# A hybrid decoder layer on one core: the per-layer-embedding product computed between the router's matmuls and kept in DRAM scratch, and the last expert pair scattered into four PSUM banks

## The reference, cut to what matters

```python
mix = jnp.concatenate([h_m, h_b], axis=-1) @ w_out[l]
x = x + mix
y = moe_ffn(rmsnorm(x, ffn_norm_g[l]), w_router[l], b_router[l], w_gate_up[l], b_gate_up[l], w_down[l], b_down[l])
x = x + y
g = jax.nn.sigmoid(rmsnorm(x, ple_norm_g[l]) @ w_ple_gate[l])
x = x + g * (p[l] @ w_ple_proj[l])

# in moe_ffn
logits = t @ w_router + b_router
top_vals, top_idx = lax.top_k(logits, 4)
gates = one_hot(top_idx) weighted by softmax(top_vals)
for e in range(32):
    hu = t @ w_gu[e] + b_gu[e]
    glu = min(hu[:, :1024], 7);  lin = clip(hu[:, 1024:], -7, 7)
    y = y + gates[:, e:e+1] * ((glu * sigmoid(1.702 * glu) * (lin + 1)) @ w_dn[e] + b_dn[e])
```

## Time and profile before

| | |
|---|---|
| three timed runs | 1172.05, 1172.11, 1172.97 us (median 1172.11) |
| profiled execution, span from first to last instruction | 1169.2 us (its own time outside the span is not recorded) |
| PE busy, share of the span | 1120.5 us, 96% |
| DVE, ACT, POOL busy | 235.3, 159.4, 20.1 us |
| bytes moved by DMA | 431.36 MB |
| chain that ended last, by engine | PE 70%, DMA 26%, DVE 1%, ACT 1%, POOL 1% |

### The profile page before, as it was taken

The page is one execution under the profiler, slowest core; times in us unless marked ns, Lnnn a source line. Parts: engine busy times, 40 slices in busy tenths (PEclk is TensorE's granted clock), DMA queues, the critical chain, the costliest instruction groups (busy, mean ns, idle before and its releaser), DMA issues.

```text
span 1169.2 us, 12153 instructions
## 1 busy us (share of the span) xinstructions
PE 1120.5 (96%) x5234; PEld 451.5 (39%) x5234; DVE 235.3 (20%) x478; ACT 159.4 (14%) x308; POOL 20.1 (2%) x44
## 2 busy tenths in 40 slices
PE   6999997999999999999999989999989899999898
PEld 3476554343434343434334333333333333333243
DVE  2364134111111111202111201111111111111021
ACT  3223313110100000001101010100000000000031
POOL 2000110000000000000000000000000000000000
PEclk9999988999999999999999999999999999999999
DMA  9932426899999999999999999999999999999940
GB/s 351 317 135 82 159 93 252 317 428 427 427 428 428 426 428 428 427 429 426 428 427 429 426 426 429 428 428 427 428 428 427 428 429 425 428 429 427 425 193 36
DMA packets 41214, 431.36 MB, mean 369 GB/s; under 512 B 5728, under 2 KB 5984, under 8 KB 16584
## 3 DMA queue, kind: packets, MB, share of 16 engines
q1 hardware_dynamic: 41104, 430.54, 88.0%
q10 hardware_dynamic: 56, 0.03, 0.0%
HBM read 429.51 MB, written 1.05 MB: 368 GB/s over the span
## 4 chain that ended last, share of the span: by engine, by line
PE 70%; DMA 26%; DVE 1%; ACT 1%; POOL 1%; issue 0%; POOLq 0%; DVEq 0%; ACTq 0%
DMA ring<-in_w_gate_up 26%; PE hu L837 24%; PE po L858 14%; PE aux L813 5%; PE hu L532 5%; PE aux L822 3%; PE hu L538 2%; PE hu L547 2%; PE hu L829 2%; PE po L850 2%; PE po L967 1%; PE hu L967 1%; PE po L844 1%; PE po L675 0%; PE aux L789 0%; PE po L894 0%
## 5 line engine op out<-in xcount | busy, mean ns | idle before, releaser
L837 PE MATMUL hu<-ring,xg_t 128*64 128x512 f32 x2048 | 466.5, 597 | 23.3 <-DMA ring<-in_w_gate_up 23.3
L837 PEld LDWEIGHTS hu<-ring,xg_t 128*64 128x64 f32 x2048 | 137.7, 136 | 329.8 <-issue 284.2
L858 PE MATMUL po<-ring,early 128*64 128x512 f32 x1024 | 226.8, 595 | 0.0
L858 PEld LDWEIGHTS po<-ring,early 128*64 128x64 f32 x1024 | 70.7, 137 | 153.9 <-issue 130.8
L1255 DVE TENSOR_SCALAR early<-hu 128x512 f32<-128x512 f32 x32 | 22.1, 692 | 463.6 <-PE hu L837 463.6
L1241 DVE TENSOR_TENSOR xt<-xt,aux 128x512 f32<-128x512 f32 x68 | 43.7, 684 | 164.5 <-PE aux L822 164.5
L822 PE MATMUL aux<-num_t,early 64*128 64x512 f32 x272 | 67.6, 615 | 0.3 <-ACT num_t L1502 0.3
L532 PE MATMUL hu<-ring 128*128 128x512 f32 x144 | 63.9, 596 | 0.0
L813 PEld LDWEIGHTS aux<-early,big 128*128 128x128 f32 x512 | 58.4, 192 | 13.0 <-issue 13.0
L813 PE MATMUL aux<-early,big 128*128 128x128 f32 x512 | 61.4, 278 | 0.0
L1494 ACT ACTIVATE early<-early 128x512 f32<-128x512 f32 x32 | 20.2, 630 | 254.0 <-DVE early L1255 254.0
(11 more groups left out here) (249 smaller groups left out, 553.9 us busy)
## 6 DMA issues: line engine op xcount, KB each, us to landing
ring<-in_w_gate_up SPq DMA_DIRECT2D x128, 2048.0 KB, 34.5
ring<-in_w_down SPq DMA_DIRECT2D x64, 2048.0 KB, 36.7
ring<-in_w_in SPq DMA_DIRECT2D x7, 2048.0 KB, 15.5
ring<-in_w_out SPq DMA_DIRECT2D x2, 2048.0 KB, 8.3
ring<-in_w_ple_gate SPq DMA_DIRECT2D x2, 2048.0 KB, 37.0
xt<-in_x SPq DMA_DIRECT2D x2, 512.0 KB, 4.1
ring<-in_w_ple_proj SPq DMA_DIRECT2D x1, 1024.0 KB, 34.0
out_x<-big SPq DMA_DIRECT2D x4, 256.0 KB, 2.0
```

Source lines behind the costliest of these rows:

```text
L837: last = mm(hu[n * SLOTS:(n + 1) * SLOTS, 2 * e + b, :], xg[:, k, e * SLOTS:(e + 1) * SLOTS], w[:, o:o + NB], start=(k == 0), stop=(k == K ...
L858: last = mm(po[n * SLOTS:(n + 1) * SLOTS, 0, :], actT[:, f, h * SLOTS:(h + 1) * SLOTS], w[:, o:o + NB], start=False, stop=(h == 1 and f == ...
```

## The change

1. `p` is transposed right after `output_transposes(1)`, into `aux`, and ScalarE copies it to SBUF (`pT`).
2. SP loads `w_ple_proj` right behind expert chunk 6 into the SBUF tile that had held the mLSTM numerators; to make it fit, `num_t` and `xg_t` become one tile `num_xg`, with the same contents at the same use.
3. `ple(0)` to `ple(3)` run between the router's matmuls, into the `hu` banks; ScalarE copies each to SBUF (`ple_s`), and SP stores the two tiles to a DRAM scratch of 1 MB behind expert chunk 8. The first up chunk waits for the four copies, the first activation for the stores.
4. At the end the order of the last loads is the two `w_ple_gate` chunks, then the scratch (1 MB) in the place of `w_ple_proj`; VectorE reads the product from there.
5. The first pair has no scatter, and GpSimd's two memsets are gone.
6. The last pair is scattered inside the loop, tile 0 into `aux` and tile 1 into `hu`, so that tile 1 no longer waits for VectorE. The gate product goes into `aux` and `hu` (`GATE_BANKS`), and its waits are split: the first four matmuls for ScalarE's columns, the next four for VectorE's.
7. ScalarE's squares and column copies at the end are interleaved.

```diff
@@ -171,8 +171,9 @@
         actT = early[:, 3072:3072 + NB].rearrange("p (f s) -> p f s", s=P)
-        out_s = num_t[:, 0:2 * NB].rearrange("p (e n) -> p e n", e=2)
-        pT = early[:, 1536:1536 + PLE // P * S].rearrange("p (k s) -> p k s", s=S)
+        out_s = num_xg[:, 0:2 * NB].rearrange("p (e n) -> p e n", e=2)
+        pT = early[:, 768:768 + PLE // P * S].rearrange("p (k s) -> p k s", s=S)
+        ple_s = [early[:, 2560:2560 + D], early[:, 1536:1536 + D]]
@@ -340,12 +343,16 @@
-        PLE_BANKS = [hu[:, 0, :], hu[:, 1, :], aux[:, 0, :], aux[:, 1, :]]
+        GATE_BANKS = [aux[:, 0, :], aux[:, 1, :], hu[:, 0, :], hu[:, 1, :]]
...
+
+        ple_d = nc.dram_tensor("ple_scratch", (S, D), F32).ap()
+        ple_dst = ple_d.rearrange("(t p) d -> t p d", p=P)
+        ple_src = ple_d.rearrange("(t p) d -> p t d", p=P)
@@ -398,6 +405,12 @@
                 load_expert(m)
+                if m == 6:
+                    sp.dma_start(w_pp, w_pp_k).then_inc(wpp_loaded, 16)
+                if m == RING - 1:
+                    for tt in range(TT):
+                        sp.wait_ge(ple_ready, HALVES * (tt + 1))
+                        sp.dma_start(ple_dst[tt, :, :], ple_s[tt]).then_inc(ple_stored, 16)
@@ -409,8 +422,10 @@
                         load_expert(m)
-            for c, (parts, src) in enumerate(((PLE // P, w_pp_k), (4, w_pg_k[:, 0:4, :]), (4, w_pg_k[:, 4:8, :]))):
+            for c, (parts, src) in enumerate(((4, w_pg_k[:, 0:4, :]), (4, w_pg_k[:, 4:8, :]), (TT, ple_src))):
                 sp.wait_ge(chunk_done, npass * PER_PASS + (MOE0 + c - RING + 1))
+                if c == 2:
+                    sp.wait_ge(ple_stored, 16 * TT)
@@ -494,10 +509,6 @@
-
-            pool.wait_ge(chunk_done, CHUNK_WO_A + 1)
-            g.memset(ghotT, 0.0).then_inc(ghotT_ready, 1)
-            g.memset(out_s, 0.0).then_inc(out_s_ready, 2)
@@ -736,6 +747,10 @@
             output_transposes(1)
+            for k in range(PLE // P):
+                for tt in range(TT):
+                    last = tr(aux[:, 1, k * S + tt * P:k * S + tt * P + P], pt_in[:, tt, k * P:(k + 1) * P], ident[:])
+            last.then_inc(pT_ps, 1)
@@ -757,6 +772,17 @@
+            def ple(q):
+
+                tt, n = divmod(q, HALVES)
+                if q == 0:
+                    pe.wait_ge(wpp_loaded, 16)
+                pe.wait_ge(xq_ready, q + 1)
+                for k in range(PLE // P):
+                    last = mm(hu[:, q, :], pT[:, k, tt * P:(tt + 1) * P], w_pp[:, k, n * NB:(n + 1) * NB],
+                              start=(k == 0), stop=(k == PLE // P - 1))
+                last.then_inc(ple_ps, 1)
@@ -764,17 +790,20 @@
             for q in range(2):
-                pe.wait_ge(x2_ready, q + 1)
+                pe.wait_ge(y_done, q + 1)
...
             w_out_part(3, range(2, 4)).then_inc(chunk_done, 1)
-            pe.wait_ge(x2_ready, 3)
+            pe.wait_ge(pT_ready, 1)
+            ple(0)
+            pe.wait_ge(y_done, 3)
...
             logit_parts(0)
-            pe.wait_ge(x2_ready, 4)
+            pe.wait_ge(y_done, 4)
...
             logit_parts(1)
+            ple(1)
@@ -782,6 +811,8 @@
                 mm(po[:, 1, b * E:(b + 1) * E], ones[:], mask[:, 0, :], start=(b == 0), stop=False, skip_group_check=True)
+            ple(2)
+            ple(3)
@@ -877,15 +908,20 @@
                     pe.wait_ge(xg_ready, ps * (2 * PAIRS) + (2 * pair + 1))
+                    if pair == 0:
+                        pe.wait_ge(y_done, ps * (QUADS * PAIRS) + QUADS)
+                        pe.wait_ge(ple_ready, QUADS)
...
                     pe.wait_ge(xg_ready, ps * (2 * PAIRS) + (2 * pair + 2))
-                    pe.wait_ge(out_s_ready, experts + (2 * pair + 2))
-                    pe.wait_ge(ghotT_ready, pairs + (pair + 1))
-                    scatter(0)
+                    if pair:
+                        pe.wait_ge(out_s_ready, experts + 2 * pair)
+                        pe.wait_ge(ghotT_ready, pairs + pair)
+                        scatter(0, aux)
                     up_chunk(0, 1, m0 + 1)
-                    pe.wait_ge(y_done, ps * (QUADS * PAIRS) + (pair * QUADS + 2))
-                    scatter(1)
+                    if pair:
+                        pe.wait_ge(y_done, ps * (QUADS * PAIRS) + (pair * QUADS + 2))
+                        scatter(1, aux)
@@ -922,50 +958,27 @@
-
-            for k in range(PLE // P):
-                for tt in range(TT):
-                    last = tr(po[:, 1, k * S + tt * P:k * S + tt * P + P], pt_in[:, tt, k * P:(k + 1) * P], ident[:])
-            last.then_inc(pT_ps, 1)
-
-            def ple(q):
-
-                tt, n = divmod(q, HALVES)
-                for k in range(PLE // P):
-                    last = mm(PLE_BANKS[q], pT[:, k, tt * P:(tt + 1) * P], final_slot(0, D, PLE // P)[:, k, n * NB:(n + 1) * NB],
-                              start=(k == 0), stop=(k == PLE // P - 1))
-                last.then_inc(pple_ps, 1)
-
-            pe.wait_ge(out_s_ready, npass * (2 * PAIRS) + 2)
-            pe.wait_ge(ghotT_ready, npass * PAIRS + 1)
-            pe.wait_ge(xg_ready, npass * (2 * PAIRS) + 2)
-            scatter(0)
-            pe.wait_ge(pT_ready, 1)
-            wait_final_chunk(pe, npass, 0)
-            ple(0)
-            pe.wait_ge(y_done, npass * (PAIRS * QUADS) + 2)
-            scatter(1)
-            ple(1)
+                pe.wait_ge(out_s_ready, experts + 2 * PAIRS)
+                pe.wait_ge(ghotT_ready, pairs + PAIRS)
+                pe.wait_ge(xg_ready, ps * (2 * PAIRS) + (2 * PAIRS + 2))
+                scatter(0, aux)
+                scatter(1, hu)
             for q in range(QUADS):
-                pe.wait_ge(y_done, npass * (PAIRS * QUADS) + max(q + 1, 2))
+                pe.wait_ge(y_done, npass * (PAIRS * QUADS) + (q + 1))
                 quad_transposes(q, QUAD_BANKS[q])
-                if q == 1:
-                    pe.wait_ge(y_done, npass * (PAIRS * QUADS) + 4)
-                    ple(2)
-            ple(3)
...
                 tt, n = divmod(q, HALVES)
-                if n == 0:
-                    pe.wait_ge(hT_act, 12 + 4 * tt)
-                    pe.wait_ge(hT_dve, 6 + 4 * tt)
...
                     if q == 0 and k % 4 == 0:
-                        wait_final_chunk(pe, npass, 1 + k // 4)
-                    last = mm(QUAD_BANKS[q], x3T[:, k, tt * P:(tt + 1) * P],
-                              final_slot(1 + k // 4, D, 4)[:, k % 4, n * NB:(n + 1) * NB],
+                        wait_final_chunk(pe, npass, k // 4)
+                    if n == 0 and k == 0:
+                        pe.wait_ge(hT_act, 12 + 4 * tt)
+                    if n == 0 and k == 4:
+                        pe.wait_ge(hT_dve, 6 + 4 * tt)
+                    last = mm(GATE_BANKS[q], x3T[:, k, tt * P:(tt + 1) * P],
+                              final_slot(k // 4, D, 4)[:, k % 4, n * NB:(n + 1) * NB],
@@ -1276,20 +1289,23 @@
-                    for tt in range(TT):
-                        dve.wait_ge(scatter_ps, ps * (TT * PAIRS) + (pair * TT + tt + 1))
-                        add_y(tt)
-                    dve.wait_ge(y_done, ps * (QUADS * PAIRS) + (pair * QUADS + QUADS))
+                    if pair:
+                        for tt in range(TT):
+                            dve.wait_ge(scatter_ps, ps * (TT * PAIRS) + ((pair - 1) * TT + tt + 1))
+                            add_y(tt, aux)
+                        dve.wait_ge(y_done, ps * (QUADS * PAIRS) + (pair * QUADS + QUADS))
+                    else:
+                        dve.wait_ge(ple_stored, 16 * TT)
...
-
-            for tt in range(TT):
-                dve.wait_ge(scatter_ps, npass * (PAIRS * TT) + (tt + 1))
-                add_y(tt)
+                for tt in range(TT):
+                    dve.wait_ge(scatter_ps, ps * (TT * PAIRS) + ((PAIRS - 1) * TT + tt + 1))
+                    add_y(tt, hu if tt else aux)
+                dve.wait_ge(y_done, ps * (QUADS * PAIRS) + (QUADS * PAIRS + QUADS))
@@ -1309,8 +1325,9 @@
                 dve.wait_ge(fin_sig, q + 1)
-                dve.wait_ge(pple_ps, q + 1)
-                v.tensor_tensor(quad(xs, q), quad(lin2, q), PLE_BANKS[q], ALU.mult).then_inc(fin_step, 1)
+                if q == 0:
+                    wait_final_chunk(dve, npass, 2)
+                v.tensor_tensor(quad(xs, q), quad(lin2, q), quad(final_slot(2, D, TT), q), ALU.mult).then_inc(fin_step, 1)
@@ -1443,6 +1460,8 @@
             output_tile(1)
+            act.wait_ge(pT_ps, 1)
+            a.copy(pT.rearrange("p k s -> p (k s)"), aux[:, 1, :]).then_inc(pT_ready, 1)
@@ -1474,6 +1493,12 @@
                 a.activation(gates[:, tt, :], lg[:, tt, :], ACT.Exp, bias=stat[:, 32 + tt:33 + tt]).then_inc(route_exp, 1)
+                if tt == 1:
+                    act.wait_ge(mask_ready, TT)
+                for n in range(HALVES):
+                    q = tt * HALVES + n
+                    act.wait_ge(ple_ps, q + 1)
```

(23 more changed lines are left out.)

32 lines of the change are left out of this document (17 added, 15 removed).

## The result

The changed kernel takes **1158.02 us** (median of four runs, 1157.85 to 1159.74); the kernel before, timed beside it, 1172.54 (1172.05 to 1173.8, four runs). The ratio is 0.988 [0.9864, 0.9895]: 14.5 us less.

A forecast was written before the change was run, and what follows sets the result against it. It took the expert weight stream to set the pace in the second half, so only the ends count. Router 0.2, stream's start 2.2 and end 6.9 make 9.3 us: span 1159.9, forecast 1162.8 us, range 1160.0 to 1167.5.

The forecast's parts named there:

- The end: Behind the last gate_up chunk: four embedding products go and scatters no longer wait; 6.9 us less, bounds 5.5 and 7.3.
- the step on VectorE's additions: At the end: additions take 1.28 us a tile, so the fourth quad is ready just as TensorE has transposed three.
- The stream's start: Expert chunks 9 to 14: without pair 0's scatters, chunks are issued sooner; 2.2 us less, bounds 0.8 and 3.2.
- The rival of the unmoved stream: First chunk gaps come from the DMA engines, not late issues; only the end counts, 1165.2 us; chance 0.07.
- that of added bytes: 2.1 MB more before chunk 9 cost 2.5 us per MB in the stream; 1167.8 us; chance 0.05.
- The router: Up to chunk 9: insertions and a held clock net 0.2 us earlier, between 1.3 earlier and 1.0 later.
- The clock: Router's first gather: added products keep TensorE at 2.4 GHz, so 4.98 us becomes 3.77; 1.2 us back.
- the insertions fit and the clock holds: Router's favourable bound: the first pair's gather done 1.3 us earlier.
- The insertions: Router: the transposes of `p` and the products `ple(0)` to `ple(3)` start the first gather 1.0 us later.
- The load: Router: `w_ple_proj` lands at 187.2 us, behind chunk 6 at 184.6, its wait hidden to within 0.1.
- One sign of being wrong: Listed in advance: the prediction is wrong if `ple(0)` in the router waits for its weights.
- the distance of 2.9 us from span to median: Whole kernel: median 1172.1 us lies 2.9 above the profiled span 1169.2; the same was added to 1159.9.

The follow-up runs named there:

- the first pair of profiles: The profiled execution of the kernel before that the prediction read (span 1169.2 us) and the first profile of the changed kernel (span 1156.1 us).
- experiments 5: Kernel before without the scatter of zeros in the first pair, nothing else: 1169.88 us, ratio 0.9985.
- experiment 6: Changed kernel with the first pair's scatter of zeros and the two memsets put back: 1163.1 us, ratio 0.992.
- Experiment 7: Kernel before with the four embedding products at the end left out, waits and banks kept: 1169.48 us, ratio 0.998.
- 8: Changed kernel with the last pair's two scatters both into the aux banks, the second waiting for VectorE: 1161.87 us, ratio 0.9904.
- 9: Changed kernel with the gate product again waiting for all eight columns of a tile at its start: 1161.31 us, ratio 0.9908.
- 11: Changed kernel with its last pair reordered: gather earlier, half of each scatter behind the last up product, x's columns before the squares: 1158.45 us, ratio 0.9887.
- the execution of the rows: The one profiled execution of the kernel before from which the prediction was made: span 1169.2 us.
- the copy: Kernel before run again without an edit: 1173.28 us, ratio 1.0007.
- the other pair: Profiles of both kernels run again without an edit: span 1172.6 us for the kernel before, 1158.3 for the changed one.
- experiment 4: Changed kernel run again without an edit: 1160.32 us, ratio 0.9895.
- the filler alone: Kernel before with eight matmuls that nobody reads at the four places in the router where the change puts the embedding product: 1169.73 us, ratio 0.9983.

## Why the prediction was too careful

**The end: right, by its steps.** 6.9 was forecast and 7.3 measured. The first gate matmul stands 5.75 behind the scatter's start, where 6.0 was reckoned. Products alone would have given 4.1: the four banks and the split wait pay for most of the rest (1.7 and 0.8), as the step on VectorE's additions supposed.

**The stream's start: right, a little small.** 2.2 said, 2.7 in both pairs of profiles, and 3.0 and 2.3 by itself. Chunk 14 is issued at 226.47 and lands 12.0 later, at 238.5. From chunk 9's landing that is 25.8 us, where the earlier trace rows had 27.9: 2.1 of the 2.7 lie where the step put them. The stream's own pace did not move (175 chunks in 862.6 us, 4.93 each). The rival of the unmoved stream falls by experiments 5 and 6, that of added bytes by this pace and by the window from 200 to 205 above, in which the DMA engines are 0.01 busy: the added bytes were through before chunk 9.

**The router: the step that failed.** It was "net 0.2 earlier", between 1.3 earlier and 1.0 later. From the second output transposes to the first expert matmul the first pair of profiles differs by 1.0, still inside these bounds, and the second by 3.4. More profiles can be read for this stretch, since the edits of experiments 5 and 7 lie behind it, and those of 6, 8, 9 and 11 too. It took 29.64 (the execution of the rows), 31.99, 31.89 and 30.61 us in the four of the kernel before, and 28.55 to 29.08 in the six with the change. The means are 31.0 and 28.7: 2.4 less and not 0.2, and outside the bounds. Its two terms:

- *The clock, where the error is.* Said: 1.2 back, from a gather of 4.98. That holds for the execution that was read, but the prediction took it for the program, and it was the shortest of four. In the copy the gather takes 6.5 and the steps before it 0.9 longer, so that holding 2.4 GHz gives 2.6 at the gather and not 1.2. The upper bound, "the insertions fit and the clock holds", was made from the same execution and so was no bound.
- *The insertions.* Said: 1.0 later. The gather starts 0.24 later. In that lie 0.65 of insertions, less 0.41 that the position counts ahead of it gain by the clock (0.46 us from the first of them to the gather, for 0.87). The transposes of `p` cost 0.44, as reckoned (0.45). The load was right: 2.6 behind chunk 6 said (187.2 and 184.6), 2.7 measured (182.3 and 185.0, from 171.99 and 13.0); it stands earlier in time because chunk 6 does. One sign of being wrong did come true: `ple(0)` waited 0.79 us for its weights. It cost 0.2, as TensorE had idled there before. From the page of the changed kernel:

```profile
num_xg<-in_w_ple_proj SPq DMA_DIRECT2D x1, 1024.0 KB, 13.0
```

  The Trainium skill (DMA: Bandwidth & Descriptors, Measured) gives 6.15 us for 1 MB, for a transfer issued from GpSimd. Behind a transfer in flight on SP's queue this one needed 2.7, so here the page's figure doesn't serve as the distance between two landings.

**What no step held, and luck.** The prediction put the stretch ahead of the change at nothing. In the first pair of profiles it is 2.5 us shorter, the largest single part of the miss, and 1.25 in the other pair, with an unchanged program. The other profiles show that most of this is a draw. The second output transposes start between 171.84 and 175.47 in the five programs that are the kernel before up to there, and between 171.73 and 175.07 in seven that are the changed one. Experiment 7, a kernel before:

```profile
171.84 0.60 PE L702 MATMUL po<-ident,big 128*128 128x128 f32 x4
```

The granted clock falls there in zero, one or two places between 140 and 175: in two in four of the five, and in four of the seven. The means, 174.4 and 173.8, are 0.6 apart; whether the change has a hand in so little stays open. And the distance of 2.9 us from span to median, which was kept, was partly such a draw: in the copies a run's time is 1.7 to 2.2 above its own span; the missing 1.0 was an execution quicker than the median. The changed kernel has 1.75 between its own two numbers.

Added up for the first measurement: 9.3 forecast; 0.8 more in the router, 2.5 ahead of it, 0.5 and 0.4 at the stream's two ends, less 0.4 behind the gates; and 1.4 from the median of before, 1172.5, against the 1171.1 that its profiled execution stands for (1169.2 and the 1.9 of the copies), less 0.2 on the changed kernel's side. That is 14.3, for 14.5 measured. Part of the first measurement's miss of 4.8 is luck. The ten runs of the changed kernel taken together (the first four and the six of experiment 4) have a median of 1159.9, which is 12.2 below the 1172.1 of all runs of the kernel before. That is 2.9 more than the forecast's 9.3, and most of it is the router's 2.4 for 0.2.

The sign and its chance were right. The range was not. Its lower end, 1160.0, lies 0.3 below all its own best cases together (7.3, 3.2 and 1.3 from 1172.1 make 1160.3). So it held nothing for a clock other than that of the one execution, in the router or ahead of it.

## What to carry over

Read a stretch in which TensorE has gaps in more than one execution before pricing it: one profile's granted clock is a draw, and here the same 32 instructions took 5.0 or 6.5 us. A matmul put into such a gap can have a negative price, and a test for it is cheap, both ways: put in work that nobody reads, and take the useful work out. Where the middle of a kernel is set by a stream, cut the trace at the stream's first free issue and last landing: here it kept its length within 0.6 us in eight profiles of the changed kernel (895.42 to 896.02, all but experiment 6's), whatever was done at its ends, and each end could be checked by itself.

## What the runs showed that was not expected

- The time of an unchanged program scatters by 6 us (1168.9 to 1175.0) with the granted clock of the records (0.994 to 0.989), and most of it arises between 140 us and the issue of chunk 9, where TensorE has gaps of up to 3.6 us: that issue lies between 207.3 and 212.1 in four profiles of the kernel before or of one that differs from it only further behind, while the stretches behind it repeat within 0.5 us in the two pairs of the table. With the change the router's own part of this is gone (28.55 to 29.08 us in six profiles, for 29.64 to 31.99). With the gaps filled the runs lie closer: 1167.8 to 1170.8 with the filler alone, 1157.9 to 1160.8 with the change.
- Leaving 7.5 us of TensorE's work out made the kernel 2.6 us slower.
- 1 MB queued behind a 2 MB chunk landed 2.7 us after it, close to the stream's rate (half of 4.93), although by then only these two were in flight.
